# A seventh place for weight pieces, and a new order of late loads and roundings, in a two-block hybrid kernel

## The reference

```python
o = rms_norm_2(o, out_norm_g) * jax.nn.silu(zf)
y_d = o.reshape(bsz, seq_len, V_WIDTH).astype(h.dtype) @ w_delta
merged = jax.nn.sigmoid(gate_f) * y_f + jax.nn.sigmoid(gate_d) * y_d
return merged @ w_out
...
h = h + hybrid_mixer(...)
h = h + hierarchical_moe(...)      # 64 experts, top 2 of one group
```

## Time and profile before

| | us |
|---|---|
| median of 3 runs | 1165.97 (1164.84 to 1210.38) |
| the profiled execution's own time | 1162.76 |
| its span, first to last instruction | 1160.6 |
| busy: PE / DVE / ACT / POOL | 1006.2 / 509.5 / 380.8 / 427.6 |
| bytes moved | 304.74 MB, mean 263 GB/s |

### The profile page before, as it was taken

One profiled execution on the slowest core, in us unless ns is written; L12 is line 12 of the kernel. 1 busy time (PEld: TensorE's weight loads), 2 busy tenths in 40 slices (PEclk: granted clock), 3 DMA queues, 4 the chain that ended last, 5 costly groups with the idle time before them and its releaser, 6 DMA issues.

```text
span 1160.6 us, 20096 instructions
## 1 busy us (share of the span) xinstructions
PE 1006.2 (87%) x8121; PEld 794.6 (68%) x8121; DVE 509.5 (44%) x977; ACT 380.8 (33%) x572; POOL 427.6 (37%) x192
## 2 busy tenths in 40 slices
PE   8999999999999998999989989976667666666686
PEld 6999999999999998798989887432223232322231
DVE  4356965601136887768864734222222222222213
ACT  5554353444447556334343525100000000000002
POOL 6767868888876756333031351000000000000000
PEclk9999999999999999999999999988888888888899
DMA  7645546566656445125211878999999999999995
GB/s 251 219 129 153 176 128 183 180 183 187 188 172 212 149 124 165 54 57 218 77 71 56 303 313 375 401 428 427 427 430 427 430 428 426 430 427 427 430 422 223
DMA packets 43568, 304.74 MB, mean 263 GB/s; under 512 B 5092, under 2 KB 5476, under 8 KB 30952
## 3 DMA queue, kind: packets, MB, share of 16 engines
q1 hardware_dynamic: 43208, 303.21, 69.0%
q10 hardware_dynamic: 288, 0.52, 0.1%
HBM read 302.67 MB, written 1.05 MB: 262 GB/s over the span
## 4 chain that ended last, share of the span: by engine, by line
PE 50%; DMA 27%; DVE 14%; issue 3%; ACT 2%; POOL 2%; SPq 2%; DVEq 0%; ACTq 0%; POOLq 0%
DMA arena<-gate_up 24%; PE bank L491 10%; PE bank L493 10%; PE bank L492 10%; PE bank L1368 6%; PE bank L1389 3%; PE bank L876 2%; DVE arena L2355 2%; DMA arena<-down 1%; DVE arena L2102 1%; POOL rounded L2938 1%; DMA arena<-front 1%; DVE arena L2554 1%; DVE arena L2552 1%; SPq L3023 1%
## 5 line engine op out<-in xcount | busy, mean ns | idle before, releaser
L2938 POOL TENSOR_TENSOR rounded<-weights,rounded 128x1024 fp32r<-128x1024 f32 x152 | 370.4, 2463 | 159.6 <-ACT rounded L1454 150.2
L491 PE MATMUL bank<-rounded 128*128 128x256 f32 (+2 forms) x776 | 219.5, 283 | 3.1 <-POOL rounded L2938 2.3
L492 PE MATMUL bank<-rounded 128*128 128x256 f32 (+2 forms) x776 | 216.7, 279 | 0.0
L493 PE MATMUL bank<-rounded 128*128 128x256 f32 (+2 forms) x776 | 216.5, 279 | 0.0
L1454 ACT ACTIVATE rounded<-weights 128x1024 fp32r<-128x1024 f32 x146 | 147.2, 1052 | 81.6 <-PE bank L493 50.3
L491 PE MATMUL bank<-rounded,rounded 128*128 128x256 f32 (+3 forms) x552 | 159.0, 288 | 3.3 <-DVEq L2357 1.6
L492 PE MATMUL bank<-rounded,rounded 128*128 128x256 f32 (+3 forms) x552 | 156.5, 284 | 0.0
L493 PE MATMUL bank<-rounded,rounded 128*128 128x256 f32 (+3 forms) x552 | 156.5, 283 | 0.0
L491 PEld LDWEIGHTS bank<-rounded 128*128 128x128 f32 (+1 forms) x776 | 145.4, 187 | 5.6 <-POOL rounded L2938 2.7
L493 PEld LDWEIGHTS bank<-rounded 128*128 128x128 f32 (+1 forms) x776 | 145.4, 187 | 0.0
L492 PEld LDWEIGHTS bank<-rounded 128*128 128x128 f32 (+1 forms) x776 | 145.2, 187 | 0.3 <-issue 0.2
(11 more groups left out here) (467 smaller groups left out, 1434.7 us busy)
## 6 DMA issues: line engine op xcount, KB each, us to landing
weights<-front SPq DMA_DIRECT2D x164, 512.0 KB, 4.2
arena<-down SPq DMA_DIRECT2D x31, 2048.0 KB, 21.9
weights<-gate_up SPq DMA_DIRECT2D x28, 2048.0 KB, 34.6
arena<-gate_up SPq DMA_DIRECT2D x28, 2048.0 KB, 33.6
weights<-front SPq DMA_DIRECT2D x4, 2048.0 KB, 8.1
weights<-gate_up SPq DMA_DIRECT2D x8, 768.0 KB, 13.1
arena<-gate_up SPq DMA_DIRECT2D x4, 1536.0 KB, 33.6
arena<-front SPq DMA_DIRECT2D x4, 512.0 KB, 5.8
```

What stands on the lines that cost most here:

```text
L491: nc.tensor.matmul(out, a[0], b[1], start=start, stop=False)
L492: nc.tensor.matmul(out, a[0], b[0], start=False, stop=False)
L493: return nc.tensor.matmul(out, a[1], b[0], start=False, stop=stop)
L2938: nc.gpsimd.tensor_tensor(lo, raw[q % RAW], hi.bitcast(f32), ALU.subtract).then_inc(sem("w_lo"), 1)
```

## The change

A seventh set is added at `squares_at = meta_at + 1104`, which is column 34224 to 36272 of `arena`, where the squares of the normalisation of the queries were and which lies inside `odd[3]` (32472 to 36568). Piece 3 goes there. It is loaded right after piece 2, behind waits for `w5_f` and `w5_b`, and rounded between the two squares of the output. From piece 4 on the pieces go round the other six sets, one later than before. The roundings in the loop over j become: `sum_hi(0)`, 7, 8, `sum_hi(1)`, 9, 10, `sum_hi(2)`, 11, 12, `sum_hi(3)`, 13. In the SP queue odd block 2 stands after piece 9 as before; then come pieces 10 and 11, odd block 3, and pieces 12 to 15. Even block 2 now waits for piece 13.

```diff
-        N_PARTS, PART_SETS = 16, (0, 1, 5, 4, 2, 3, 0, 1, 4, 2, 3, 0, 1, 4, 2, 3)
-        PART_IN = {0: "slot0_in", 1: "second_in", 2: "slot1_in", 3: "small_in", 4: "ws_in", 5: "consts_in"}
+        N_PARTS, PART_SETS = 16, (0, 1, 5, 6, 4, 2, 3, 0, 1, 4, 2, 3, 0, 1, 4, 2)
+        PART_IN = {0: "slot0_in", 1: "second_in", 2: "slot1_in", 3: "small_in", 4: "ws_in", 5: "consts_in", 6: "res_in"}
         N_HALVES = 2 * ZB
-        PART_BEFORE = {0: whole_in(2), 1: 16 * 5, 2: whole_in(3), 3: 16 * 6, 4: 16, 5: 16}
+        PART_BEFORE = {0: whole_in(2), 1: 16 * 5, 2: whole_in(3), 3: 16 * 6, 4: 16, 5: 16, 6: 16}
...
-        part_at = [2 * i * QUARTER for i in range(4)] + [RING + home_at, RING + query_at]
-        hi_at = [at + QUARTER for at in part_at[:5]] + [RING + key_at]
-        set_raw = [weights[:, at:at + QUARTER] for at in part_at[:4]] + [arena[:, at:at + QUARTER] for at in (home_at, query_at)]
+        squares_at = meta_at + 1104
+        assert squares_at + 2 * QUARTER <= free_from
+        part_at = [2 * i * QUARTER for i in range(4)] + [RING + home_at, RING + query_at, RING + squares_at]
+        hi_at = [at + (key_at - query_at if i == 5 else QUARTER) for i, at in enumerate(part_at)]
+        set_raw = [weights[:, at:at + QUARTER] for at in part_at[:4]] + [arena[:, at:at + QUARTER] for at in (home_at, query_at, squares_at)]
...
             out_squares(0)
             round_part(2)
+            round_part(3)
             out_squares(1)
...
             for j in range(4): delta_hi(j)
-            for n in (3, 4, 5): round_part(n)
+            for n in (4, 5, 6): round_part(n)
             for j in range(4):
                 sum_hi(j)
-                round_part(2 * j + 6)
                 round_part(2 * j + 7)
+                if j < 3:
+                    round_part(2 * j + 8)
...
-                if n >= 6:
+                if n >= 7:
                     part_done(part_last(n))
...
             load_part(2)
+            sp.wait_ge(sem("w5_f"), 2)
+            sp.wait_ge(sem("w5_b"), 2)
+            load_part(3)
             sp.wait_ge(sem("o_b"), 4)
...
             sp.wait_ge(full[fills["no"].b], fills["no"].n + 1)
-            load_part(3)
+            load_part(4)
             last = readers[f"block{GD + 1}"]
             sp.wait_ge(full[last.b], last.n + 1)
-            load_part(4)
             load_part(5)
+            load_part(6)
             load_down_first(0, 0)
-            load_part(6)
             load_part(7)
+            load_part(8)
             load_down_second(0)
-            load_part(8)
             load_part(9)
             load_gate_up(1, 1, [2])
-            for n in range(10, 14): load_part(n)
+            load_part(10)
+            load_part(11)
             load_gate_up(1, 1, [3])
-            load_part(14)
-            load_part(15)
+            for n in range(12, N_PARTS): load_part(n)
             sp.wait_ge(sem("merged2"), 4)
             load_gate_up(0, 0, [1])
             load_gate_up(1, 1, [1])
-            part_done(12)
+            part_done(13)
             load_gate_up(0, 0, [2])
             part_done(15)
             load_gate_up(0, 0, [3])
```

## The result

The changed kernel takes 1174.98 us (median of 4 runs, 1174.66 to 1175.61) against 1166.61 before. The ratio is 1.0078, 95% interval [1.0055, 1.0101], so it is 9.1 us slower (the ratio is of fast runs; it leaves out the one slow run of the kernel before, at 1210.38, which is in that median). The forecast was slower by 4.9 us: the direction is right and the size is about half of what came.

What follows compares the result with a forecast made beforehand. The expert loop was taken as a saturated weight stream whose end follows PE's arrival. Piece 9 -2.5 us, `sum_hi(3)` +6.4 and clock +1.0 gave +4.9, from 1165.97 to 1170.9 us; range 1163.5 to 1175.5.

Steps and rivals of the forecast that it cites:

- The frame: Expert loop: a saturated weight stream ends a fixed time after PE arrives; the start of `wp1` moves the end.
- Roundings against the queue: ACT ahead of `wp1`: `sum_hi(2)` and `sum_hi(3)` stand behind roundings of pieces that follow blocks; +6.4 us for `sum_hi(3)`.
- faster: Rival at the queue: blocks don't hold small pieces, sums come in time, `wp1` 3.6 us earlier, 1162.4 us; chance 0.12.
- The clock: Last pair of `wp0`: after PE stands still 5.0 us, 2.1 us of work at half speed; +1.0 us, ends 0 and 2.4.
- heavier: Rival: PE's gaps pull the clock down longer, 2.5 to 3 us instead of 1.0, 1173.5 us; chance 0.15.
- Round 3 and its rest: POOL and DVE at L2704: a second POOL operation delays `wd0` to `wd3` by 2.1 us; nothing in the sum.
- Odd block 3 earlier: SP queue after 682 us: the block moves into an empty stretch, prefetch still ends in time; costed at nothing.
- The hole: Empty stretch of the queue from 682 us, where piece 13 waited for `wp0`; the block was to fill it, 4.95 us.
- The sum: Start of `wp1`, carried to the end: -2.5 us for piece 9, +6.4 for `sum_hi(3)`, +1.0 for low clock, together +4.9.
- The lighter rival: Queue ahead of piece 9 runs ahead, piece 12 lands up to 2.4 us earlier, 1168.5 us; chance 0.16.

Runs made afterwards that it cites:

- e2: Changed kernel with all sums on ScalarE ahead of the roundings that wait for a block; ratio to the kernel before 1.0015 [0.9998, 1.0033].
- e3: Changed kernel with odd block 3 back behind piece 13 in the queue, roundings as changed; ratio to the kernel before 1.0036 [1.0017, 1.0055].
- e5: Changed kernel with only the last sum moved, to stand behind round 11 and ahead of round 12; ratio to the kernel before 1.0016 [0.9992, 1.004].
- e10: Changed kernel with five unread products in TensorE's wait ahead of the last pair of `wp0`; ratio to the kernel before 1.0066 [1.0043, 1.009].
- e1: The kernel before, run again with no edit; ratio to the kernel before 0.999 [0.9968, 1.0011].
- e4: Changed kernel with round 3 behind the square root of the output norm; ratio to the kernel before 1.006 [1.0041, 1.008].
- e6: Changed kernel with all sums ahead of the waiting roundings and round 3 behind the square root; ratio to the kernel before 0.9991 [0.997, 1.0011].
- e8: Kernel before with only odd block 3 moved up behind piece 11, ScalarE order as before; ratio to the kernel before 0.9977 [0.9957, 0.9997].
- e9: The changed kernel, run again unchanged; ratio to the kernel before 1.0098 [1.0074, 1.0123].

## Why the prediction was right or wrong

*The frame* held: the distance from the loop's start to the end stayed fixed, and only PE's arrival counted. But "whatever [the start of `wp1`] moves by, the end follows" is 1.1 us short: `wp1` was forecast at 81.2 and started at 81.8, and from there to the loop it took 37.8 us instead of 36.7.

*Roundings against the queue.* Right in mechanism and size. In times from piece 0's load, `sum_hi(2)` was forecast at 70.6 and ran at 71.0, `sum_hi(3)` at 78.1 and 78.5. e2 took 5.4 us off by this order alone. The rival 'faster', in which small pieces overtake a block, is refuted by the 5.14 and 4.94 us of waiting. What the prediction didn't see is the second path from `sum_hi(2)` to `sum_hi(3)`, over DVE (e3, e5); in the changed kernel it isn't the one that ends last.

*The clock* is the step that failed by size: the prediction laid the one low stretch of the trace before, 3.4 us, on the new wait and let it end with the last pair of `wp0`, "1.0 us more". e10 measures about 2.0. The low stretch here is 6.8 us (0.96, 0.50, 0.50, 0.50, 0.84 in five windows of 2 us), and it reaches 1.7 us into `wp1`. The upper end that was stated, 2.4 us from the earlier trace rows, was the right row to take. PE stood still twice within 10 us here, 1.87 and 4.80 us. That two waits are needed for the longer stretch is not so: e1 has 6.8 us behind a single wait of 3.21. As to the clock the rival 'heavier', which had 0.15, was right.

*Round 3 and its rest* is the step that failed by its reason. The 2.1 us on DVE came out as 2.0, but "it costs nothing in the sum ... still stand in a full queue" doesn't hold: e4 and e6 show 2.0 and 2.6 us. I had checked that the pieces' issue times come ahead of their landings, and not that the queue stays full until the next issue. Nor do the losses of the clock ahead of `wd0` "fall where PE waits anyway": they delay the issue of pieces 7 and 8 by 0.8 us in the first trace and by some 2.5 in e2, e3 and e5.

*Luck.* That `sum_hi(3)` came only 0.4 us later than forecast is two errors that cancel. In e4, without the cost of round 3, it runs at 77.1, a microsecond ahead of the forecast. The forecast had taken 63.3 for piece 9 from the one trace of the kernel before; in e4 it is rounded at 62.1, and in e1 the piece in that place (8) is rounded at 62.1 too. The lateness of round 3 made up for it.

*Odd block 3 earlier* at nothing: right as to the block (e8), as long as no sum stands behind it. The hole was not filled, it moved.

*The sum.* In the trace D grew by 6.6, forecast 4.9. Of the 1.7 between them 0.6 stand ahead of `wp1` (0.4 from the sum, 0.2 from the clock) and 1.1 behind it (0.8 from the clock, 0.3 not traced). The measured ratios stand for 9.1 and 11.4 us. The profiled pair shows 12.0 us, of which 5.8 is scatter ahead of piece 0. What remains open is the 2.5 to 4.5 us between D's growth and the timed difference: over the runs the ratio moves about 1.4 times as much as D of the one trace that each has. The clock is the likeliest place, not a shown one. The record has each run's mean granted clock: 0.934 on average in e9's six runs against 0.940 in the 17 of the kernel before beside them, and 0.938 in e10's. Within e9 time and clock go together, from 1172.23 at 0.936 to 1178.96 at 0.931, and the profiled execution was the fastest of the six. Only the profiled ones have a trace, so where in the kernel the others were low can't be seen.

*The lighter rival* had the queue run ahead; it ran nearly dry instead, and only in e4, where `wd0` is in time, is the last sum a microsecond early.

## What to carry to other kernels

An engine that works in order and both receives data and serves another engine should do the serving first: before a rounding is moved, read what its transfer stands behind in the queue and what stands behind the rounding on its engine. Where one queue is the limit, check that it is never empty, not only that each issue comes ahead of its landing. Follow every path into such a step, also one over a third engine: here DVE's order ties the last sum to the one before it. And when a wait of TensorE becomes longer, add the work behind it at half speed for as long as the longest low stretch seen, not the nearest; one trace of the kernel before showed 3.4 us and another 6.8, so take two.

## What the runs showed of the hardware

The stand-still of two DVE operations with both inputs in SBUF beside POOL's subtraction was nearly a full one: 2.0 us for one more POOL operation, where one alone took 2.37. Waits of TensorE of 1.9 to 4.8 us were mostly followed by a granted clock of 0.50, for 3.4 us or 6.8 (some 10 in e9, with a second wait inside), and the length didn't follow the wait: 3.4 behind 4.41 and 6.8 behind 3.21 in two traces of one program. A wait of 2.87 us in e8 left it at 1.00. Five products that nobody reads, 4.5 us of work, took about 2 us off the path: with them in the wait the granted clock stayed at 1.00. And the first 610 us of unchanged code scatter by 7 us, about half of it seen in the clock, which is more than the whole local effect of this change: without the cut at piece 0's load the profiled pair would have put 12 us down to it.
